# A two-layer diffusion backbone: norm sums moved off TensorE, output projections in two column halves

## The reference: what is computed

```python
hx = modulate(rms_norm(x, norm1_g[l]), sh1, sc1)
zx = hx @ w_in[l]
a_x = rwkv_output(...)            # bidirectional delta-rule scan, width 1024
b_x = conformer_branch(...)       # gated, depthwise convolution, layer_norm, silu, width 512
c_x = sgu_branch(...)             # gelu, layer_norm, mixing in chunks of 128 tokens, width 512
x = x + g1 * merge(zx, (a_x, b_x, c_x), w_merge[l])
x = x + g2 * swiglu(modulate(rms_norm(x, norm2_g[l]), sh2, sc2), ffn_w_in[l], ffn_w_out[l])
...
return rms_norm(x, final_norm_g)  # latent tokens only
```

## Time and profile before

| | |
|---|---|
| median of the runs | 4349.19 us |
| the profiled execution | 4361.62 us, span of the core 4359.8 us |
| TensorE matmuls busy | 4146.8 us (95%), granted clock 0.981 of full |
| VectorE, ScalarE busy | 1354.8 us (31%), 1072.7 us (25%) |
| GpSimd busy | 58.1 us (1%) |
| DMA | 260.34 MB, 60 GB/s over the span |
| first phase | 0 to 51.9 us |
| layer 0: lora and pairs, branches, res1, ffn, res2 | to 1063, 1658, 1758, 2215, 2459 us |
| layer 1: the same | to 3419, 3819, 3886, 4190, 4360 us |

### The profile page before, as it was taken

One profiled execution on the slowest core, in us unless ns is written; L12 is line 12 of the kernel. 1 busy time (PEld: TensorE's weight loads), 2 busy tenths in 40 slices (PEclk: granted clock), 3 DMA queues, 4 the chain that ended last, 5 costly groups with the idle time before them and its releaser, 6 DMA issues.

```text
span 4359.8 us, 107588 instructions
## 1 busy us (share of the span) xinstructions
PE 4146.8 (95%) x50580; PEld 2420.8 (56%) x50580; DVE 1354.8 (31%) x2123; ACT 1072.7 (25%) x1783; POOL 58.1 (1%) x52
## 2 busy tenths in 40 slices
PE   7999999989999999999999988999998899999998
PEld 3566666666455555555555546666665444444443
DVE  2655555555710000100000145555554310010000
ACT  3444444432110000100000244454443120010000
POOL 0000000000000000000000000000000000000000
PEclk9999999999999999999999989999998999999999
DMA  5000000103412111111111200000001442212222
GB/s 192 24 8 23 23 23 23 33 21 125 160 64 97 55 52 50 44 53 49 53 53 53 84 25 8 22 22 22 22 31 32 169 145 78 77 64 77 77 82 72
DMA packets 67383, 260.34 MB, mean 60 GB/s; under 512 B 7680, under 2 KB 9984, under 8 KB 66048
## 3 DMA queue, kind: packets, MB, share of 16 engines
q1 hardware_dynamic: 62208, 219.18, 15.3%
q10 hardware_dynamic: 3456, 29.04, 1.6%
q0 software_dynamic: 1280, 5.24, 0.3%
HBM read 239.80 MB, written 13.63 MB: 58 GB/s over the span
## 4 chain that ended last, share of the span: by engine, by line
PE 90%; ACT 4%; issue 3%; DMA 2%; DVE 1%; SPq 0%; ACTq 0%; DVEq 0%
PE psum L632 37%; PE psum L973 15%; PE psum L1340 12%; PE psum L857 11%; PE psum L869 5%; PE psum L1005 2%; PE psum L623 2%; PE psum L817 2%; DMA ring<-w_stream_in 2%; PE psum L740 1%; PE psum L835 1%; PE psum L760 1%; ACT L1391 1%; ACT arena L1729 0%; ACT arena L1722 0%
## 5 line engine op out<-in xcount | busy, mean ns | idle before, releaser
L632 PE MATMUL psum<-arena,ring 128*128 128x512 f32 (+1 forms) x4432 | 1600.3, 522 | 2.0 <-DMA ring<-w_stream_in 1.2
L632 PEld LDWEIGHTS psum<-arena,ring 128*128 128x128 f32 x4432 | 840.2, 190 | 770.3 <-issue 722.2
L973 PEld LDWEIGHTS psum<-arena 32*32 32x32 f32 (+3 forms) x40512 | 703.7, 118 | 368.7 <-issue 281.9
L973 PE MATMUL psum<-arena 32*32 32x32 f32 (+4 forms) x40512 | 795.5, 209 | 111.8 <-issue 65.4
L857 PE MATMUL psum<-arena,ring 128*128 128x512 f32 (+1 forms) x1408 | 575.2, 525 | 4.7 <-ACT arena L1541 1.6
L1340 PE MATMUL psum<-arena,ring 128*128 128x512 f32 (+1 forms) x1440 | 520.2, 521 | 0.0
L1340 PEld LDWEIGHTS psum<-arena,ring 128*128 128x128 f32 x1440 | 273.6, 190 | 242.0 <-issue 229.5
L857 PEld LDWEIGHTS psum<-arena,ring 128*128 128x128 f32 x1408 | 242.5, 192 | 165.3 <-issue 135.4
L2354 DVE TENSOR_TENSOR arena<-psum,arena 128x768 f32<-128x768 f32 (+1 forms) x44 | 36.3, 825 | 718.9 <-PE psum L632 687.2
L2296 DVE TENSOR_TENSOR arena<-psum,arena 128x768 f32<-128x768 f32 (+1 forms) x48 | 39.6, 825 | 605.8 <-PE psum L632 605.8
L1856 ACT ACTIVATE arena<-psum 128x768 f32<-128x768 f32 (+1 forms) x44 | 31.0, 704 | 698.8 <-PE psum L632 677.2
(11 more groups left out here) (123 smaller groups left out, 2560.7 us busy)
## 6 DMA issues: line engine op xcount, KB each, us to landing
ring<-w_stream_in SPq DMA_DIRECT2D x408, 512.0 KB, 3.6
x_spill<-arena ACTq DMA_DIRECT2D x2, 3072.0 KB, 8.7
arena<-ya_spill ACTq DMA_DIRECT2D x2, 3072.0 KB, 10.3
arena<-x_spill ACTq DMA_DIRECT2D x2, 3072.0 KB, 18.2
ring<-w_stream_in ACTq DMA_DIRECT2D x8, 512.0 KB, 6.2
arena<-x_in ACTq DMA_DIRECT2D x1, 3072.0 KB, 14.1
arena<-ups_in SPq DMA_DIRECT2D x16, 192.0 KB, 2.4
ya_spill<-arena POOLq DMA_DIRECT2D x8, 384.0 KB, 5.7
```

Of the source, the lines that this page charges most:

```text
L632: mm = eng.matmul(psum[0:lhs[k].shape[-1], tile, a - off:b - off], lhsT=lhs[k], rhs=rhs[k][:, a:b], start=(k == 0), stop=(k == len(lhs) - ...
L973: return pe.matmul(out, lhsT=lhs, rhs=rhs, start=start, stop=stop, skip_group_check=True)
```

## The change

It has four parts.

**Sums of squares.** For the five RMS norms VectorE adds the eight squared tiles (`add_square`, seven additions for each column half), and TensorE's `norm_sum` is one matmul with ones for each half, where it was eight tiles of both. For the layer norms GpSimd adds the four tiles (`summed`, three additions for each of four sums), and `smean`, `svar`, `cmean` and `cvar` are products with one tile.

**Column halves.** `out_phase` and `project_two` go first over the columns up to 512 (`CUT`) and then over columns 512 to 768. In `out_phase` all eight output tiles of the first half come first, so `w_merge` and `ffn_w_out` are streamed twice: 8 chunks of res1 become 16, 24 of res2 become 48. The norm of the first half (`norm_rsqrt`, `normed`, `modulated`, `last_scaled`) is issued among the steps of the second.

**Loads of the branch phase.** The scan output and the parameters are loaded after the second `sv` tile, x after the gate `g00`, where all four loads stood at the start.

**Pair turns.** All `WEAVE` strings are replaced by others of the same number of each letter.

```diff
-    "dxdxxssxsdsxxssxdxdddxddsdsdddsxdddsdddsdddxdsdddsddssdddsddsdddsdddsxdsdddsdddsdddsxddddsddssdsdsss"
-    "sdsssssdsssdddsdsdsdssssssssssssssssssssssdsssssss")) for t in range(2, KT))
+    "xxdsxsdssdxxssxdxxdddxsddsdsdddsxddddsddxdsddddsddsddsdsddsxddsdddsddsdddsdddsddddsddsdxddsdddsdsdssss"
+    "sddssdsssdsssddsdssdssssssssssssssssssssssdsssssss")) for t in range(2, KT))
...
+        def side_cols(c0, h):
+            return ((c0, CUT), (CUT, T))[h]
...
-            for k in range(KT):
-                eng.wait_ge(*ready(k))
-                for x in range(2):
-                    for a, b in halves(c0, c0):
+            for h in range(2):
+                a, b = side_cols(c0, h)
+                for k in range(KT):
+                    eng.wait_ge(*ready(h * KT + k))
+                    for x in range(2):
                         last[x] = eng.matmul(...)
...
-                    if q >= KT:
-                        norm_sum(0, q - KT, 2, 0)
+                    if q == FIRST_SUMS:
+                        for h in range(2):
+                            norm_sum(0, h, 2, 0)
...
+            def norm_sum(n, h, tile, c0):
+                a, b = side_cols(c0, h)
+                pe.wait_ge(*sqa.at(n, (h + 1) * (KT - 1) - 1))
+                pe.matmul(psum[:, tile, CUT * h:CUT * h + b - a], lhsT=ones, rhs=slot(H0, a, b), ...)
...
                     elif name == "smean":
-                        pe.wait_ge(*A.at(f"sv{CT - 1}"))
-                        mm = project(pe, tile, [ones] * CT, [slot(SV + i) for i in range(CT)], c0, c0)
+                        pe.wait_ge(*G.at(f"sa{CT - 1}"))
+                        mm = project(pe, tile, [ones], [slot(H1 + 1)], c0, c0)
...
-                for j in range(KT):
-                    tile = j % 3
-                    take(tile, V.at(f"x{j}", l))
+                for i in range(2 * KT):
+                    h, j = divmod(i, KT)
+                    tile = i % 3
+                    a, b = side_cols(c0, h)
+                    take(tile, V.at(f"x{h}{j}", l))
...
+                    if i == KT + 1:
+                        norm_sum(NORMS[norm], 0, 3, NORM_FROM[norm])
+                norm_sum(NORMS[norm], 1, 3, NORM_FROM[norm])
...
+                norm_rsqrt(0, (0, 1), 2, 0)
                 act.wait_ge(*S.at(f"m0.{MOD_ITEMS - 1}"))
                 mod_copy(0)
-                norm_rsqrt(0, 2, 0)
...
-                act.dma_start(arena[:, YA0 * T:(YA0 + KT) * T], ya_spill).then_inc(s_back, 16)
-                act.dma_start(arena[:, X0 * T:(X0 + KT) * T], spill).then_inc(s_back, 16)
-                act.dma_start(sgu_w, ...)
-                act.dma_start(sgu_b, ...)
...
                     gelu("sv", SV, j)
+                    if j == 1:
+                        act.dma_start(sgu_w, ...)
+                        act.dma_start(sgu_b, ...)
+                        act.dma_start(arena[:, YA0 * T:(YA0 + KT) * T], ya_spill).then_inc(s_back, 16)
...
+                act.dma_start(arena[:, X0 * T:(X0 + KT) * T], spill).then_inc(s_x, 16)
                 gate("g10")
...
+                for i in range(2 * KT):
+                    h, j = divmod(i, KT)
+                    act.wait_ge(*phases[which]["V"].at(f"x{h}{j}", l))
+                    square(i, c0)
+                    if i == KT:
+                        norm_rsqrt(n, (0,), 3, c0)
+                        tables(LOG)
+                    if scales is not None and KT < i <= KT + 4:
+                        modulated(n, 0, scales, c0, 2 * (i - KT - 1), 2 * (i - KT))
+                norm_rsqrt(n, (1,), 3, c0)
+                if scales is not None:
+                    modulated(n, 1, scales, c0)
...
+            def add_square(n, i, c0):
+                h, j = divmod(i, KT)
+                if j:
+                    dve.wait_ge(*sq.at(n, i))
+                    dve.tensor_tensor(slot(H0, a, b), slot(H0, a, b), slot(H0 + j, a, b), ALU.add).then_inc(sqa.sem, 1)
...
+                    ins.then_inc(*V.mark(f"x{h}{j}"))
+                    if i:
+                        add_square(m, i - 1, c0)
+                    if KT < i <= KT + 4:
+                        scaled(m, 0, c0, 2 * (i - KT - 1), 2 * (i - KT))
+                add_square(m, 2 * KT - 1, c0)
+                scaled(m, 1, c0)
...
+                def summed(name, ready, total, tiles):
+                    for j in range(1, CT):
+                        pool.wait_ge(*ready(j - 1))
+                        pool.wait_ge(*ready(j))
+                        first = tiles[0] if j == 1 else total
+                        pool.tensor_tensor(slot(total, c0), slot(first, c0), slot(tiles[j], c0), ALU.add)...
...
-        for j in range(KT):
+        for j in list(range(KT)) * 2:
             put(tile(x["w_merge"][l], j * P))
```

More of the change, by code:

```diff
@@ L174 @@
[L174 to L178, removed]
@@ L192 @@
[L192 to L195, removed]
-WEAVE.update((("V", 1, t), "tssstttssstpsssssssppspsssssppsssssppspssstsspspsppssssppppssspsppppppsssssssssssssssssss") for t in (1,))
@@ L754, in mod_turn @@
                 mm.then_inc(modt.sem, 1)
-            def norm_sum(n, j, tile, c0):
-                pe.wait_ge(*sq.at(n, j))
-                for a, b in halves(c0, c0):
-                    mm = pe.matmul(psum[:, tile, a - c0:b - c0], lhsT=ones, rhs=slot(H0 + j, a, b),
-                                   start=(j == 0), stop=(j == KT - 1), skip_group_check=True)
-                if j == KT - 1:
-                    mm.then_inc(nsum.sem, 1)
+            def norm_sum(n, h, tile, c0):
+                a, b = side_cols(c0, h)
+                pe.wait_ge(*sqa.at(n, (h + 1) * (KT - 1) - 1))
+                pe.matmul(psum[:, tile, CUT * h:CUT * h + b - a], lhsT=ones, rhs=slot(H0, a, b),
+                          start=True, stop=True, skip_group_check=True).then_inc(nsum.sem, 1)
             def first_phase():
@@ L1835, in branch_phase, with squares @@
                     act.dma_start(par[:, :], par_in[l + 1, :, :]).then_inc(s_par, 16)
-            def squares(which, l, norm):
+            def squares(which, l, norm, scales):
                 tables(LOG)
-                for j in range(KT):
-                    act.wait_ge(*phases[which]["V"].at(f"x{j}", l))
-                    square(j, NORM_FROM[norm])
-                norm_rsqrt(NORMS[norm], 3, NORM_FROM[norm])
+                c0, n = NORM_FROM[norm], NORMS[norm]
+                for i in range(2 * KT):
[4 more added lines that the diff above has]
+                        norm_rsqrt(n, (0,), 3, c0)
+                        tables(LOG)
+                    if scales is not None and KT < i <= KT + 4:
+                        if i == KT + 1 and scales:
+                            act.wait_ge(*modr.at(mod_thirds(l)[1], 1))
+                        modulated(n, 0, scales, c0, 2 * (i - KT - 1), 2 * (i - KT))
+                norm_rsqrt(n, (1,), 3, c0)
+                if scales is not None:
+                    modulated(n, 1, scales, c0)
             def ffn_phase(l):
@@ L2357, in _ @@
             dve.wait_ge(s_load, 48)
+            for i in range(2 * KT):
+                add_square(0, i, 0)
+            normed(0, 0, 0)
             mod_ready(0)
-            normed(0, 0)
+            normed(0, 1, 0)
             for l in range(DEPTH):
```

227 lines of the change are left out of this document (127 added, 100 removed).

## The result

The changed kernel takes 4251.14 us (median of four runs, 4249.27 to 4258.02) beside 4351.56 us of the kernel before on the same chip (median of four runs, one more than in the table above). The ratio is 0.9774 with a 95% interval of 0.9757 to 0.9791, 98 us less by the ratio; the forecast was 88 us less, 4261 us. The profiled execution took 4249.73 us with a span of 4247.9. The profiled execution of before lay some 10 us above its median, so the two traces are 112 us apart where the medians are 100 apart.

The account below looks back on a forecast made before the run. The prediction took TensorE as the bound, its matmuls busy 4146.8 of 4359.8 us. Gains of 52 + 6.5 + 24 + 5.5 = 88 us led to 4261 us, own range 4240 to 4282, with rivals 4236 to 4292.

Parts of the forecast that it names:

- Norm sums and halves: Output phases and the end: fewer sum matmuls and an early first-half norm save 17.0, 16.4, 11.5 and 7 us, together 52.
- The clock rival: The 1.7 us gap before `project_two` brings the low clock, 8 us in all over three `project_two`, giving 4269; chance 0.10.
- First phase: Kernel start through the first `project_two`: seven sum tiles go, additions and multiplications precede `mod_ready`; 6.5 us less, between 3 and 9.
- Layer-norm sums: Branches of both layers: four sums per layer lose three of four tiles, against waits for GpSimd; 24 us less.
- From `smean` to the first transposition: Layer 0 branches: the stretch from `smean` to the first transposition falls from 27.8 us to 21.
- The GpSimd rival: Branches: GpSimd's additions take twice as long beside VectorE, and VectorE's taps longer too; 16 us, giving 4277; chance 0.06.
- Loads: Branches: moving the loads gains 6 us in layer 1 and costs 0.5 in layer 0; 5.5 us less in sum.
- the load landing of 17 us is gone or falls to 12: Layer 1 branches: a chunk's load that took 17.17 us to land no longer does, or takes 12.
- Pair turns: New strings in 16 scan turns: no sign can be told, so 0 us, with -12 to +12 kept.
- middle pair turns last 107 to 111 us: Sign for the scan: middle pair turns, 109.0 us before in layer 0, stay within 107 to 111, otherwise the prediction is wrong.
- the new orders bring time, 25 us or more: Rival for the pair turns: the new strings save 25 us or more, giving 4236 or below; chance 0.08.
- Weights twice: Output phases: streaming 64 more chunks, 33 MB, costs nothing; rival at 96 us, giving 4357, has chance 0.02.

Follow-up runs that it names:

- `norm_on_pe`: The changed kernel, halves kept, with the RMS-norm sums back on TensorE, a matmul with ones behind each output tile: 4284.68 us, ratio 0.9838 to the kernel before.
- `late_first_half`: The changed kernel with the first half's norm issued behind all output tiles, sums still on VectorE: 4264.93 us, ratio 0.9794 to the kernel before.
- `ln_on_pe`: The changed kernel with the layer-norm sums back on TensorE and no additions on GpSimd: 4270.98 us, ratio 0.9804 to the kernel before.
- `loads_at_start`: The changed kernel with all four loads back at the start of the branch phase: 4254.25 us, ratio 0.9764 to the kernel before.
- `new_order_only`: The kernel before with only the WEAVE strings of the changed kernel: 4327.73 us beside 4355.06, ratio 0.9936.
- `pieces_items`: `pieces` with four modulation items instead of six behind `smean` and `svar`, a third behind each of four products: 4268.71 us, ratio 0.9801 to the kernel before.
- `pieces`: The changed kernel with the scan output's reload cut in six from the branches' start, parameters behind the last: 4239.08 and 4245.79 us, ratios 0.9735 and 0.9727.

## Why the prediction was right, point by point

- **Norm sums and halves, 52 us.** Measured 51.0 in the two traces (17.0, 16.3, 11.1, 6.6). The prices per instruction, the 1.7 us gap (1.5 measured, then 0.5 for the sum) and the cover of the second half's norm held. `norm_on_pe` and `late_first_half` split it: some 27 us are the sums' own instructions in the output phases and some 20 the early first half; the smaller additions and the warm clock are in the latter.
- **The clock rival.** It didn't happen: the clock is 1.00 behind an idle gap of 1.49 us.
- **First phase, 6.5.** Measured 6.2 in the two traces, 4.6 with the changed kernel's second profile.
- **Layer-norm sums, 24 us.** Measured about 19: 12.9 from `cmean` and `cvar` as worked out, some 5 in layer 0's first stretch where 7 stood, and in layer 1's, where 4 stood, 4 in the first trace but no more than 1 on average over the profiles. The run `ln_on_pe` says 13 by the ratios and 20 by the medians. The step that failed is the term "From `smean` to the first transposition ... I expect 21". I took the six items as a fixed length and saw that they wait for chunks, and still let the whole gain through; the ring refills during the sums, so a shorter sum makes the items behind it wait longer. The GpSimd rival was right in its mechanism and wrong in its price: VectorE is the one that slows, in slack.
- **Loads, 5.5 us.** About 0: `loads_at_start` is level. By the delay of the products, the loss in layer 1 fell from 11.9 to 9.2 us and the one in layer 0 rose from 1.3 to 3.3. I had put 6 us on the new wait in layer 1, and it was 9.2. The sign "the load landing of 17 us is gone or falls to 12" failed too: the wait in the chain is 13.27 us in layer 1 and 14.25 in layer 0. On the page of the changed kernel the scan output lands in 14.1 us where it took 10.3. (3 MB in 10.3 us are 305 GB/s when counted as the chunks were, not 290; nothing hangs on it.)
- **Another small loss in layer 0.** The last pair turn of the new orders ends with 3.84 us of waiting for VectorE (L2180) and the first branch product runs 12.28 us where 10.5 is usual. It is in the new orders (`new_order_only` has the same wait of 3.8), on TensorE's path.
- **Pair turns, 0.** The failed step: 24 to 28 us by experiment. "I can tell no sign" was fair from the rows, but the bound of 12 was not. The prediction took 4.75 us, the idle time of one middle turn, as the most that each of 16 turns could give, 76 us, and then kept a sixth of it for no reason that a row gives. That turn was among the least idle: over the pair turns TensorE stood for 140.6 us before, 81.8 of them in layer 1, and 111 of them at the scan's line, of which the new orders leave 83. By its own sign, "middle pair turns last 107 to 111 us", the prediction is wrong here: two starts of GpSimd's spill, a turn apart, are 106.1 us apart in the changed kernel:

```profile
559.96 0.54 POOL L2435 DMA_DIRECT2D ya_spill<-arena  x1 [108.26 <-DVE arena L2180]
666.09 0.54 POOL L2435 DMA_DIRECT2D ya_spill<-arena  x1 [105.59 <-DVE arena L2180]
```

  The sign was badly drawn as well: turns of the kernel before last up to 114.4 us. The rival "the new orders bring time, 25 us or more", which had 0.08, came true in its mechanism; its total of 4236 did not, because the branches gave less.
- **Weights twice.** 64 chunks more, 33.6 MB, and no wait for the ring in any output phase: TensorE's idle time at L1352 is 0.0 us on the page, and res1 and res2 of layer 0 are to 0.1 us what was forecast from the instructions. The page has the chunk's landing still at 3.6 us.

That the sum came within 10 us is in part luck: branches and loads were 10 us too high and the orders some 26 too low, two errors against each other. Earned is the part on the output phases, more than half of the gain, which was counted instruction by instruction. The forecast's own range was added wrongly, too: 18 us on either side of 4261 are 4243 to 4279, not 4240 to 4282; the measured time lies in both.

## What to carry to other kernels

Where an engine is busy 95% of the span and the phases meet in a serial chain, splitting the last step in column halves and starting the next phase on the first half turns the chain into cover; it can be priced to a microsecond from two spacings in the chain of waits. A sum taken off the bound engine is worth its instructions only if what stands behind it was waiting for that engine: in the stretch behind `smean` loads stood there, and part of the gain went into them. Schedules written out by hand for several engines are one object: TensorE's string of a better one alone kept nothing of its gain, and their worth can't be read from the strings, only bounded by the idle time at their lines. A large reload beside a ring of small chunks belongs in pieces, spread over the time before it is needed. And a stage that waits for loads has to be profiled more than once before a few us in it are called a gain.

## What the runs showed of the hardware

- A GpSimd addition of 128 x 768 beside VectorE's taps: the taps take 2.65 times their time (11.00 against 4.15 us for eight), the addition 1.2 times (2.21 against 1.80).
- An idle gap of TensorE of 1.49 us left the clock at full speed; one of 5.30 us was followed by a granted clock of 0.50, and one of 4.51 us by a `project_two` of 23.66 us where 20.64 is its time at full speed. In between it goes either way: behind the gap of 1.96 us before `smean` the sum took 1.53 us in both profiles of the changed kernel and 2.81 in `pieces_items`. This window of the changed kernel lies behind the gap of 5.30 us:

```profile
3407.00:3412.00 5.00, 4.95 (x8) 1.70 (x9) 0.00 (x0) 0.60 (x1) 0.00 (x0) 0.50 0.94 356
```

- TensorE's idle time without a releaser, at dense runs of 32-wide matmuls, depends on the order of the pieces (67.7 and 70.7 us in the two traces with the old strings, 51.0 to 60.4 in ten with all the new). What it is stays open; no run here took it apart.
- The same kernel differs by 18 us from one profiled execution to another (spans of 4247.9 and 4265.6): 11 in the pair turns and 6 in the branches of layer 1, with the output phases equal to 0.1 us. Stages of two traces tell more than their spans, where the stage is one that doesn't vary.
- 3.75 MB issued at once, the reload of 3 MB among them, delayed the products behind it by 9.2 us in layer 1 (the reload took 14.1 us to land); in six loads of 384 and 768 KB, which landed in 4.8 and 5.8 us, it delayed no product.
- The best version here is `pieces`, at 0.9727 to 0.9735 of the kernel before.
